# Second projection of a dense MLP as a Strassen block product over token, hidden and model halves

## Chip, cores and metric

The kernel runs on one core of one Trainium2 chip. The metric is the device time of one execution in microseconds (us), the median of several runs. TensorE (PE) multiplies, VectorE (DVE) and ScalarE (ACT) work elementwise, GpSimd (POOL) does small vector work and issues some transfers, SyncE (SP) issues most transfers.

## The reference, cut to what matters

Two blocks follow each other. The first has two layers, each with its mixers and then a dense MLP; the second has its own mixers and a mixture of experts. The change touches the MLP of the two layers of the first block, on 256 tokens, 1024 model columns and 4096 hidden columns (FF), all in fp32:

```python
def hybrid_layer(x, ...):            # twice
    ...
    x = x + mix @ w_out
    h2 = rms_norm(x, g_mlp_norm)
    x = x + jnp.square(jax.nn.relu(h2 @ w_up)) @ w_down   # w_up 1024x4096, w_down 4096x1024
    return x
```

The second block also needs, for each of its two layers, the product of a vector `c` with `ada_w` (1024x6144). It does not depend on x.

## The kernel before

**Tiles.** Tokens are two tiles t of 128. The MLP goes through eight units u of 512 hidden columns. For a unit, `mlp_up` (L815) fills PSUM banks 4 and 5 with the hidden values, transposed (hidden columns on partitions): 4 column groups of 128, 8 steps k each. ACT applies relu (L1558) and squares (L1560) into `uT`, a double buffer in `work`. `mlp_down` (L828) then adds this unit's share to the four PSUM banks 0 to 3, one for each token tile t and model half of 512 columns: 4 steps k for each bank, so 16 matmuls of 128x128 by 128x512. Each fp32 matmul stands in the trace as two instructions. The model rows are scaled by `rr` and added to `xres` only after all eight units.

**Order.** `MLP_ORDER` is up 0, up 1, down 0, up 2, down 1, ..., up 7, down 6, down 7; within an engine everything runs in the order it is written. Before down 7 PE does two small things: `ada_sum` (L838) and some transposes of parameter rows (L992, L993 in layer 1).

**Weights.** A unit of weights is 2 MB. Five slots of `ring` (0 to 4) hold them in turn; SP issues a load (L490) when the unit that used the slot five places earlier is done.

**What DVE does meanwhile.** In both layers DVE computes one half of the `ada_w` product during the MLP: 12 blocks c of 512 columns. A block is 1024x512 values, 2 MB, in two halves of 1 MB in slot 5 of the ring. POOL issues each half (L688) as soon as DVE is through with the one before in that place (semaphore `ada_acc`). For a block DVE does one TENSOR_SCALAR (L2223), seven SCALAR_TENSOR_TENSOR (L2225), a transpose (L2237, or L2235 for four blocks) and a reduction (L2239). At the end of the MLP it adds the product to `xres` (L2259 for tile 0, L2263 and L2265 for the halves of tile 1).

**After layer 1** the second block begins: DVE takes sums of squares (L1984), POOL makes the factor from them (L705, L707), ACT scales tile 0 (L1599) and DVE tile 1 (L1996), PE transposes both (L1020) and starts on the second block's first projection (L1042). POOL writes some constants for the second block (L695 to L697) once the semaphore `x_done` is at 5, which it is before the MLP of layer 1 begins.

Of the kernel before, what the change touches and what calls it, by code (L numbers as in the profile page):

```python
# [9 lines left out]
ALU = mybir.AluOpType  # L10
# [19 lines left out]
RING1, UNIT = 5, 4096  # L30
ROWS_BANK = (3, 7)
U_QK, U_R0, U_R1, U_R2, U_V, U_LORA, U_O, U_OUT, U_MLP = 0, 1, 2, 3, 4, 5, 6, 7, 9
UNITS1 = 25
MLP_ORDER = [("up", 0)] + [x for u in range(1, 8) for x in (("up", u), ("down", u - 1))] + [("down", 7)]
# [86 lines left out]
def first_and_second_block(nc, a, out, stop=None, dbg=None):  # L121
# [8 lines left out]
    with ctx:  # L130
# [17 lines left out]
        trig = first_only(8 * TT * 24).rearrange("p (i t j) -> p i t j", i=8, t=TT)  # L148
        ada_bias = first_only(L2 * 48).rearrange("p (l n) -> p l n", l=L2)
# [26 lines left out]
        def take(n, place=None):  # L176
# [32 lines left out]
        uT = work[:, 0:2048].rearrange("p (b c s) -> p b c s", b=2, c=4)  # L209
        ru = work[:, 2048:3072].rearrange("p (b n) -> p b n", b=2)  # L210
        ada_w = [ring[:, 5, 0:2048].rearrange("p (k n) -> p k n", k=4), ring[:, 5, 2048:4096].rearrange("p (k n) -> p k n", k=4)]
        ada_acc = work[:, 3072:4096].rearrange("p (b n) -> p b n", b=2)
        rr = sb("rr", [P, TT])[:, :]
        ada_t = work[:, 4096:4608]
        ada_red = work[:, 4608:4608 + 192].rearrange("p (c b) -> p c b", c=12)
# [5 lines left out]
            "consts", "pool_own", "params_p", "params_first", "cols_ps", "cols_sb", "x_in", "x_half", "xT_filled", "xT_act", "xT_dve", "diag_r", "rbc_filled", "out_half", "down_half", "tokens_pos", "trig_dve", "trig_act", "cond_act",  # L221
# [5 lines left out]
            "up_filled", "up_square", "down_done", "ada_acc", "ada_red", "ada_filled",  # L227
            "dve_own", "act_own", "passed", "stored")}
        ada_in = [sem("ada_in0"), sem("ada_in1")]
# [14 lines left out]
        def slot(j):  # L244
            return ring[:, j % RING1, :]

        def wide(j, n, k=DT):
            return slot(j)[:, 0:k * n].rearrange("p (k n) -> p k n", k=k)

        uq = slot(U_LORA)[:, 0:3 * 384].rearrange("p (k n) -> p k n", k=3)  # L250
        ukv = slot(U_LORA)[:, 1152:1152 + 1024].rearrange("p (k n) -> p k n", k=2)


# [18 lines left out]
        def unit_done(l, p):  # L272


            first, p = (0, p + UNITS1) if p < 0 else (1, p)
            if p < U_OUT:
                return "job_filled", NJ * l + JOB[{U_QK: "qk1", U_R0: "r01", U_R1: "r11", U_R2: "r21", U_V: "v1", U_LORA: "lkv1", U_O: "o1"}[p]] + 1
            if p < U_MLP:
                return ("out_filled", l + 1) if p == U_OUT else ("out_half", 4 * l + 4)
            kind, u = MLP_ORDER[p - U_MLP]  # L280
# [31 lines left out]
        rowsA = region(0, 128)  # L312
        rowsB = region(128, 128)
# [55 lines left out]
        landed2 = landed + [sem("landed5")]  # L369
        base2 = [16 * L1 * (UNITS1 // RING1 + (1 if r == U_LORA % RING1 else 0)) for r in range(RING1)] + [0]  # L370
# [52 lines left out]
        def _(sp):  # L423
# [43 lines left out]
            for l in range(L1):  # L467

                loads = [(wide(U_QK, 512), w_in[l, :, :, 0:512])]
# [4 lines left out]
                for i, (kind, u) in enumerate(MLP_ORDER):  # L474
                    loads.append((wide(U_MLP + i, 512), w_up[l, :, :, 512 * u:512 * u + 512]) if kind == "up" else
                                 (wide(U_MLP + i, 1024, 4), w_down[l, u]))
# [240 lines left out]
        def _(pe):  # L717
# [88 lines left out]
            def mlp_up(l, i, u):  # L806
                unit(l, U_MLP + i)
                w = wide(U_MLP + i, 512)
                for b in range(2):
# [7 lines left out]
                    if b == 0:  # L817
                        last.then_inc(s["up_filled"], 1)
# [1884 lines left out]
```

## Time and profile before

| | us |
|---|---|
| median of 3 runs | 2043.9 (2043.49 to 2044.44) |
| span of the profiled execution, first to last instruction | 2039.9 |
| PE busy in it | 1983.3 (97%) |
| DVE busy in it | 900.6 (44%) |
| ACT busy in it | 375.7 (18%) |
| POOL busy in it | 89.3 (4%) |

The profile gives the profiled execution's span; what lies around it (loading, the end) is the difference of some 4.0 us to the median. The chain of work that ended last runs over PE for 91% of the span: 11% on L815 (the first projection), 11% on L828 (the second). The idle time of an engine matters only where it stands on this chain. In the rows below, starts are us from the start of the span; "ns" stands where a duration is in ns.

### The profile page before, as it was taken

The numbers are of one execution on the slowest core, as the hardware profiler recorded it, in microseconds if no ns is written. First come the engines' busy times: TensorE is split into PE (matmuls) and PEld (weight loads), VectorE is DVE, ScalarE is ACT, GpSimd is POOL, SyncE is SP. The second block draws the span as 40 slices with busy tenths as digits, with TensorE's granted clock in tenths as the row PEclk, the third lists the DMA queues.
The fourth block names the chain that finished last, engine by engine and source line by source line (L and its number), as shares of the span: only waits on it lengthen the run. The fifth ranks groups of instructions, "written<-read, shape, count | busy, mean of one in ns | idle before, by whom it ended". The sixth has DMA issues, their size and how long they took to land.

```text
span 2039.9 us, 21592 instructions
## 1 busy us (share of the span) xinstructions
PE 1983.3 (97%) x8174; PEld 1097.2 (54%) x8174; DVE 900.6 (44%) x1828; ACT 375.7 (18%) x783; POOL 89.3 (4%) x167
## 2 busy tenths in 40 slices
PE   8999999999999999899999999989998999999997
PEld 5556666545666658654444344447765443444442
DVE  3354561245354419866777665661525110011102
ACT  2321000033100001122111111112342211111111
POOL 1121110001111000000000000000000000000000
PEclk9999999999999999989999999999999999999999
DMA  7327885333488733549999999993244999999995
GB/s 269 143 98 268 312 319 203 137 124 124 162 316 321 283 133 115 198 166 409 428 428 428 428 427 429 426 370 122 99 165 165 408 409 427 428 426 427 426 427 237
DMA packets 111572, 593.12 MB, mean 291 GB/s; under 512 B 16887, under 2 KB 21494, under 8 KB 85110
## 3 DMA queue, kind: packets, MB, share of 16 engines
q1 hardware_dynamic: 98422, 541.48, 66.1%
q0 software_dynamic: 13056, 50.33, 6.5%
q8 instruction: 66, 1.08, 0.2%
q14 instruction: 28, 0.23, 0.0%
HBM read 590.74 MB, written 1.05 MB: 290 GB/s over the span
## 4 chain that ended last, share of the span: by engine, by line
PE 91%; DMA 3%; DVE 3%; POOL 1%; issue 1%; ACT 1%; SPq 0%; POOLq 0%; DVEq 0%; ACTq 0%
PE bank L1169 31%; PE bank L815 11%; PE bank L828 11%; PE bank L1042 7%; PE bank L751 6%; PE bank L1160 5%; PE bank L1144 5%; DMA ring<-in_moe_w_up 3%; PE bank L954 3%; PE bank L1062 2%; PE bank L863 1%; PE bank L1312 1%; PE bank L1152 1%; POOL rstd L678 1%; PE bank L1330 1%
## 5 line engine op out<-in xcount | busy, mean ns | idle before, releaser
L1169 PE MATMUL bank<-ring,work 128*64 128x512 f32 x2336 | 634.8, 595 | 6.0 <-DMA ring<-in_moe_w_up 5.9
L1169 PEld LDWEIGHTS bank<-ring,work 128*64 128x64 f32 x2336 | 204.4, 137 | 329.8 <-issue 329.6
L2507 DVE SCALAR_TENSOR_TENSOR work<-work 128x512 f32<-128x512 f32 x384 | 258.6, 745 | 5.1 <-DVE work L2504 5.0
L815 PE MATMUL bank<-hT,ring 128*128 128x256 f32 x1024 | 223.4, 379 | 0.7 <-ACT hT L1470 0.7
L828 PE MATMUL bank<-ring,work 128*128 128x512 f32 x512 | 222.4, 592 | 0.0
L815 PEld LDWEIGHTS bank<-hT,ring 128*128 128x128 f32 x1024 | 194.4, 190 | 32.6 <-issue 6.9
L2511 DVE SCALAR_TENSOR_TENSOR work<-work,bank 128x512 f32<-128x512 f32 x32 | 21.9, 685 | 375.2 <-ACT work L1674 375.2
L1169 PE MATMUL bank<-seventh,work 128*64 128x512 f32 x400 | 176.1, 593 | 0.0
L2225 DVE SCALAR_TENSOR_TENSOR work<-ring,seventh,work 128x512 f32<-128x512 f32 x168 | 126.3, 752 | 109.5 <-DMA ring<-in_ada_w 104.3
L828 PEld LDWEIGHTS bank<-ring,work 128*128 128x128 f32 x512 | 97.2, 190 | 115.6 <-issue 114.8
L1042 PE MATMUL bank<-hT,ring 128*128 128x256 f32 x608 | 137.8, 388 | 0.3 <-ACT hT L1584 0.3
L751 PE MATMUL bank<-ring,hT 128*128 128x512 f32 (+1 forms) x320 | 135.0, 579 | 0.0
L1042 PEld LDWEIGHTS bank<-hT,ring 128*128 128x128 f32 x608 | 117.7, 195 | 19.5 <-issue 3.1
L1160 PE MATMUL bank<-work 128*128 128x512 f32 x256 | 123.4, 606 | 0.0
L1169 PE MATMUL bank<-work 128*64 128x512 f32 x256 | 114.7, 594 | 0.0
L1144 PE MATMUL bank<-work,xn 128*128 128x256 f32 x448 | 99.0, 379 | 0.0
L751 PEld LDWEIGHTS bank<-ring,hT 128*128 128x128 f32 x320 | 59.8, 190 | 68.7 <-issue 68.5
L1144 PEld LDWEIGHTS bank<-work,xn 128*128 128x128 f32 x448 | 84.0, 190 | 10.8
L1169 PEld LDWEIGHTS bank<-seventh,work 128*64 128x64 f32 x400 | 54.1, 137 | 57.8 <-issue 57.6
L1558 ACT ACTIVATE work<-bank 128x512 f32<-128x512 f32 x32 | 19.1, 597 | 347.4 <-PE bank L815 347.4
L1160 PEld LDWEIGHTS bank<-work 128*128 128x128 f32 x256 | 44.0, 191 | 57.5 <-issue 56.6
L2517 DVE SCALAR_TENSOR_TENSOR work<-work,bank 128x512 f32<-128x512 f32 x32 | 22.0, 688 | 114.1 <-PE bank L1169 114.1
(391 smaller groups left out, 1743.3 us busy)
## 6 DMA issues: line engine op xcount, KB each, us to landing
ring<-in_moe_w_gate SPq DMA_DIRECT2D x54, 2048.0 KB, 17.1
ring<-in_moe_w_up SPq DMA_DIRECT2D x45, 2048.0 KB, 19.4
ring<-in_moe_w_down SPq DMA_DIRECT2D x45, 2048.0 KB, 19.0
ring<-in_ada_w POOLq DMA_DIRECT2D x48, 1024.0 KB, 9.1
ring<-in_w_up SPq DMA_DIRECT2D x16, 2048.0 KB, 12.7
ring<-in_w_down SPq DMA_DIRECT2D x16, 2048.0 KB, 9.7
ring<-in_w_in SPq DMA_DIRECT2D x10, 2048.0 KB, 7.9
seventh<-in_moe_w_gate SPq DMA_DIRECT2D x10, 2048.0 KB, 19.7
```

The costliest lines, as they stand in the source:

```text
L751: last = pe.matmul(b[:, 0:n], (hT if x is None else x)[:, k, t * P:t * P + P], w[:, k, 0:n], start=(k == kk - 1), stop=(k == 0))
L815: last = pe.matmul(B(4 + b)[:, (c % 2) * S:(c % 2) * S + S], w[:, k, c * P:c * P + P], hT[:, k, :], start=(k == 0), stop=(k == DT - 1))
L828: last = pe.matmul(B(2 * t + hf), uT[:, u % 2, k, t * P:t * P + P], w[:, k, 512 * hf:512 * hf + 512], start=(u == 0 and k == 0), stop=(u = ...
L954: last = pe.matmul(B(2 * t + hf), mT[:, 4 * u + k, t * P:t * P + P], w[:, k, 512 * hf:512 * hf + 512], start=(u == 0 and k == 0), stop=(u ...
L1042: last = pe.matmul(b[:, (c % 2) * S:(c % 2) * S + S], w[:, k, c * P:c * P + P], hT[:, k, :], start=(k == 0), stop=(k == DT - 1))
L1062: last = pe.matmul(B(2 * t + hf), x[:, 4 * u + k, t * P:t * P + P], w[:, k, 512 * hf:512 * hf + 512], start=(u == 0 and k == 0), stop=(u = ...
L1144: last = pe.matmul(b[:, (d % 2) * S:(d % 2) * S + S], xn[:, t, d * P:d * P + P], pick[:, t, :], start=(t == 0), stop=(t == TT - 1))
L1160: last = pe.matmul(B(2 * t + hf), pgT[:, t * P:t * P + P], ye[:, 512 * hf:512 * hf + 512], start=False, stop=True, skip_group_check=True)
L1169: last = pe.matmul(b[h, :], x[:, k, h], rows_of(i, j + e, k)[:, c0:c0 + 512], start=(k == 0), stop=(k == kk - 1))
L2225: ins = dve.scalar_tensor_tensor(ada_acc[:, c % 2, :], ada_w[hf][:, k, :], cond[:, kk:kk + 1], ada_acc[:, c % 2, :], ALU.mult, ALU.add)
L2507: mo.do(dve.scalar_tensor_tensor(fl(bias[:, h]), mask_b, rbt[:, bass.ds(12 * bk + h, 1)], fl(bias[:, h]), ALU.mult, ALU.add))
L2517: dve.scalar_tensor_tensor(aa, zz, 0.5, U, ALU.mult, ALU.mult).then_inc(m["a_ready"], 1)
```

## The change

The second projection is written as a Strassen (Winograd form) product of 2x2 blocks, over the halves of the tokens (the tiles t), of the hidden columns (units u and u + 4) and of the model columns. For a pair pr = 0 to 3 of units pr and pr + 4, seven products n = 1 to 7 of 4 matmuls each take the place of eight. Product n adds up over the four pairs in a PSUM bank of its own, so seven banks are taken and the eighth (bank 7) takes the hidden values.

- DVE makes the factors. For each pair, four operations on weights of 128x2048 (`weights`, the 1st reads both second-projection units, the 2nd writes in place into the ring) and four on hidden values of 128x512 (`tokens`).
- PE's order (`MLP_STEPS`): four fills (half a first-projection unit each, 16 matmuls) for pair 0; then for each next pair its four fills, between them the seven products of the pair before in the order 6, 7, 4, 5, 3, 1, 2; last the seven products of pair 3 in the order 6, 1, 5, 7, 2, 3, 4. `ada_sum` stands ahead of these last seven.
- At the end DVE puts the seven sums together and adds them to `xres`.
- The ring's six slots all hold weights, with a slot for each unit by name (`UNITS1`): first-projection units 0 to 3 all use slot 0, units 4 to 7 slot 1.
- The `ada_w` blocks come in quarters of 512 KB into four places (two in `xn`, two in `work`) instead of halves of 1 MB into two. DVE's factor operations stand among its twelve blocks: the weights of pair 0, blocks 0 and 1, tokens of pair 0, blocks 2 and 3 (3 with the weights of pair 1 after its quarters), 4 and 5, tokens of pair 1, and so on.
- POOL writes the constant columns of `qkpad` and `vext` again after layer 0. Its constants for the second block now wait for `x_done` at 6, the last addition of layer 1.

```diff
-RING1, UNIT = 5, 4096
+RING1, UNIT = 6, 4096
-MLP_ORDER = [("up", 0)] + [x for u in range(1, 8) for x in (("up", u), ("down", u - 1))] + [("down", 7)]
+UNITS1 = [("qk", 0, 1), ("r0", 1, 1), ("r1", 2, 1), ("r2", 3, 1), ("v", 4, 1), ("lora", 0, 2), ("o", 1, 1), ("out0", 2, 1), ("out1", 3, 1),
+          ("down1", 4, 1), ("up0", 0, 1), ("down5", 5, 1), ("up4", 1, 1), ("down0", 2, 1), ("down4", 3, 1),
+          ("up1", 0, 1), ("up5", 1, 1), ("up2", 0, 1), ("up6", 1, 1), ("down2", 2, 1), ("down6", 3, 1),
+          ("up3", 0, 1), ("up7", 1, 1), ("down3", 4, 1), ("down7", 5, 1)]
+FILL_BANKS = (4, 5, 6, 7, 4)
+SUM_BANK = {1: 4, 2: 0, 3: 1, 4: 2, 5: 6, 6: 5, 7: 3}
+BETWEEN = ((6, 7), (4,), (5,), (3,), (1, 2))
...
-        ada_w = [ring[:, 5, 0:2048].rearrange("p (k n) -> p k n", k=4), ring[:, 5, 2048:4096].rearrange("p (k n) -> p k n", k=4)]
+        ada_w = [xn[:, q, :].rearrange("p (k n) -> p k n", k=2) for q in range(2)]
+        ada_w += [work[:, 4096 + 1024 * q:5120 + 1024 * q].rearrange("p (k n) -> p k n", k=2) for q in range(2)]
...
+        def factors(pr, n):
+            return {1: (hidden_of(pr, 0, 0), quarter(pr, 0, 0)),
+                    2: (hidden_of(pr, 0, 1), quarter(pr, 1, 0)),
+                    3: (usum[4], quarter(pr, 1, 1)),
+                    4: (hidden_of(pr, 1, 1), wdiff[4]),
+                    5: (usum[1], quarter(pr, 0, 1)),
+                    6: (usum[2], wdiff[2]),
+                    7: (hidden_of(pr, 1, 0), wdiff[3])}[n]
...
+            kind, u = name[:-1], int(name[-1])
             if kind == "up":
-                return "up_filled", 16 * (l + first) + 2 * u + 2
-            return ("down_half", 4 * (l + first)) if u == 7 else ("down_done", 7 * (l + first) + u + 1)
+                return "up_filled", 16 * l + 4 * (u % 4) - (2 if u < 4 else 0)
+            return "sums", sums_of(l, u % 4 - 2, 2)
...
                 for c in range(12):
-                    for hf in range(2):
-                        pool.wait_ge(s["ada_acc"], 24 * l + 2 * c + hf + 1)
-                        pool.dma_start(ada_w[hf], ada_src[l, :, 4 * hf:4 * hf + 4, 512 * c:512 * c + 512]).then_inc(ada_in[hf], 16)
+                    for q in range(4):
+                        pool.wait_ge(s["ada_acc"], 48 * l + 4 * c + q + 1)
+                        pool.dma_start(ada_w[q], ada_src[l, :, 2 * q:2 * q + 2, 512 * c:512 * c + 512]).then_inc(ada_in[q], 16)
...
-            pool.wait_ge(s["x_done"], 5)
+            pool.wait_ge(s["x_done"], 6)
...
+            def mlp_sum(l, pr, n):
+
+                if n in (3, 5, 6, 7):
+                    pe.wait_ge(s["factors_ready"], 32 * l + 8 * pr + {5: 5, 6: 6, 7: 7, 3: 8}[n])
+                if n == 4:
+                    pe.wait_ge(s["factors_ready"], 32 * l + 8 * pr + 4)
+                if n in (1, 2, 3):
+                    unit(l, "down%d" % (pr if n == 1 else pr + 4))
+                x, w = factors(pr, n)
+                for k in range(4):
+                    last = pe.matmul(B(SUM_BANK[n]), x[:, k, :], w[:, k, :], start=(pr == 0 and k == 0), stop=(pr == 3 and k == 3), skip_group_check=True)
+                last.then_inc(s["sums"], 1)
...
+                for n in (3, 1, 2, 4):
+                    weights(0, n)()
+                ada_block(0)
+                ada_block(1)
+                tokens(0)
+                for pr in range(1, 4):
+                    c = 4 * pr - 2
+                    ada_block(c)
+                    ada_block(c + 1, [weights(pr, n) for n in (3, 1, 2, 4)])
+                    if pr < 3:
+                        ada_block(c + 2)
+                        ada_block(c + 3)
+                    tokens(pr)
...
+                dve.wait_ge(s["sums"], sums_of(l, 3, 2))
+                do(added(0, low, bank_of(2)))
+                dve.wait_ge(s["sums"], sums_of(l, 3, 3))
+                ins = added(0, high, bank_of(3))
+                wait()
+                ins.then_inc(s["x_half"], 1)
+                dve.wait_ge(s["x_half"], 2 * l + 2)
+                if l == L1 - 1:
+                    r[0] = squared(0, xn[:, 0, :])
+                dve.wait_ge(s["sums"], sums_of(l, 3, 4))
+                added(1, low, bank_of(4)).then_inc(s["x_done"], 1)
```

PE, where the second projection begins in layer 0; before, L815 is the first projection and L828 the second:

```order
L815 MATMUL bank<-hT,ring 128x256 [waits up_square,landed0]
L815 MATMUL bank<-hT,ring 128x256 x15
L815 MATMUL bank<-hT,ring 128x256 [waits up_square]
L815 MATMUL bank<-hT,ring 128x256 x15
L828 MATMUL bank<-ring,work 128x512 [waits up_square,landed1]
L828 MATMUL bank<-ring,work 128x512 x15
L815 MATMUL bank<-hT,ring 128x256 [waits up_square,landed2]
L815 MATMUL bank<-hT,ring 128x256 x15
```

The same place in the changed kernel, where L880 is a fill and L893 a product:

```order
L880 MATMUL bank<-hT,ring 128x256 [waits up_square,landed0]
L880 MATMUL bank<-hT,ring 128x256 x15
L893 MATMUL bank<-work 128x512 [waits factors_ready]
L893 MATMUL bank<-work 128x512 x3
L893 MATMUL bank<-work 128x512 [waits factors_ready]
L893 MATMUL bank<-work 128x512 x3
L893 MATMUL bank<-work 128x512 [waits factors_ready]
L893 MATMUL bank<-work 128x512 x3
L880 MATMUL bank<-hT,ring 128x256 [waits up_square]
L880 MATMUL bank<-hT,ring 128x256 x15
L893 MATMUL bank<-ring,work 128x512 [waits factors_ready]
L893 MATMUL bank<-ring,work 128x512 x3
```

The runs of 16 of the second projection have become runs of 4 (products 6, 7, 4, then 5), of which each waits for DVE's `factors_ready`, where the 16 waited for ACT alone.

DVE, from the factor `rr` of layer 0's MLP to the end of the first `ada_w` block, before:

```order
L2214 TENSOR_TENSOR rr<-rstd 128x2 [waits rstd_ready,stat_ready]
L2223 TENSOR_SCALAR work<-ring,seventh 128x512 [waits ada_in0,dve_own]
L2225 SCALAR_TENSOR_TENSOR work<-ring,seventh,work 128x512 [waits dve_own] x3
L2225 SCALAR_TENSOR_TENSOR work<-ring,seventh,work 128x512 [waits ada_in1,ada_acc]
L2225 SCALAR_TENSOR_TENSOR work<-ring,seventh,work 128x512 [waits dve_own] x3
L2237 STREAM_TRANSPOSE work<-work 128x512 [waits ada_acc]
L2239 TENSOR_REDUCE work<-work 128x16 [waits dve_own]
```

And in the changed kernel, from the same `rr`; `landed2` and `landed3` are the units down0 and down4:

```order
L2281 TENSOR_TENSOR rr<-rstd 128x2 [waits rstd_ready,stat_ready]
L2333 TENSOR_TENSOR work<-ring 128x2048 [waits landed3,landed2,dve_own]
L2336 TENSOR_TENSOR ring<-ring 128x4x512 [waits factors_ready]
L2341 TENSOR_TENSOR work<-ring 128x2048 [waits factors_ready]
L2346 TENSOR_TENSOR work<-ring,work 128x2048 [waits factors_ready]
L2292 TENSOR_SCALAR work<-xn,seventh 128x512 [waits ada_in0,factors_ready]
L2294 SCALAR_TENSOR_TENSOR work<-xn,seventh,work 128x512 [waits dve_own]
L2294 SCALAR_TENSOR_TENSOR work<-xn,seventh,work 128x512 [waits ada_in1,ada_acc]
L2294 SCALAR_TENSOR_TENSOR work<-xn,seventh,work 128x512 [waits dve_own]
L2294 SCALAR_TENSOR_TENSOR work<-work,seventh 128x512 [waits ada_in2,ada_acc]
```

Four operations of 128x2048 now stand ahead of the first block, behind a wait for a weight unit, and the block waits for four transfers where it waited for two.

POOL, ahead of the second block's first factor, in the changed kernel (before, the IOTA row has no other wait than `x_done` either, at a lower value):

```order
L759 IOTA work 128x32 [waits x_done]
L760 MEMSET work 128x4x2
L761 MEMSET work 128x4x30
L769 TENSOR_SCALAR stat<-stat 128x1 [waits pool_own,stat_ready_2]
L771 TENSOR_TENSOR rstd<-stat,mhalf 128x1 [waits pool_own]
```

The order of these rows is unchanged; the value waited for is that of the end of layer 1's MLP, so the first factor (tile 0) stands behind it.

## Rows read from the trace of the kernel before

**Rows 1.** The page: the span, and the busy time of DVE.

```profile
span 2039.9 us, 21592 instructions
PE 1983.3 (97%) x8174; PEld 1097.2 (54%) x8174; DVE 900.6 (44%) x1828; ACT 375.7 (18%) x783; POOL 89.3 (4%) x167
```

**Rows 2.** The chain that ended last, in both MLPs: start, us, what.

```profile
165.75 27.87 PE bank L815 x128
193.62 13.73 PE bank L828 x32
207.35 13.81 PE bank L815 x64
...
748.31 13.75 PE bank L828 x32
```

**Rows 3.** Busy time by stretch; the last columns are granted clock, DMA share, GB/s.

```profile
193.50:221.00 27.50, 27.50 (x97) 18.20 (x96) 15.68 (x23) 2.45 (x4) 2.99 (x4) 1.00 0.94 347
```

**Rows 4.** Timeline of DVE in layer 0: start, us, line, operation, idle before it.

```profile
160.12 1.22 DVE L2202 TENSOR_TENSOR xres<-xres,bank 128x1024 f32<-128x1024 f32 x1 [8.90 <-PE bank L954]
...
163.55 0.69 DVE L2206 TENSOR_TENSOR xres<-xres,bank 128x512 f32<-128x512 f32 x1 [1.03 <-PE bank L954]
...
176.44 0.48 DVE L2223 TENSOR_SCALAR work<-ring,seventh 128x512 f32<-128x512 f32 x1 [5.96 <-DMA ring<-in_ada_w]
176.96 2.33 DVE L2225 SCALAR_TENSOR_TENSOR work<-ring,seventh,work 128x512 f32<-128x512 f32 x3
182.37 3.11 DVE L2225 SCALAR_TENSOR_TENSOR work<-ring,seventh,work 128x512 f32<-128x512 f32 x4 [3.09 <-DMA ring<-in_ada_w]
185.52 0.71 DVE L2237 STREAM_TRANSPOSE work<-work 128x512 f32<-128x512 f32 x1
186.26 0.69 DVE L2239 TENSOR_REDUCE work<-work 128x16 f32<-128x512 f32 x1
...
321.03 0.69 DVE L2239 TENSOR_REDUCE work<-work 128x16 f32<-128x512 f32 x1
372.99 0.17 DVE L2249 TENSOR_TENSOR modc<-bank,seventh 32x24 f32<-32x24 f32 x1 [51.28 <-PE bank L838]
```

**Rows 5.** Timeline of POOL in layer 0: the first two issues of `ada_w`.

```profile
170.16 1.74 POOL L688 DMA_DIRECT2D ring<-in_ada_w  x2
```

**Rows 6.** Line L688: the 48 issues of `ada_w` and their time to landing.

```profile
L688 POOL DMA_DIRECT2D ring<-in_ada_w x48: 748/748/954, 170.2 to 692.9; - x48
...
DMA to landing us min/median/max: 5.5/9.1/12.0
```

**Rows 7.** Loads of `w_down` issued from 100 to 165 us.

```profile
L490 SPq DMA_DIRECT2D ring<-in_w_down x1: 368/368/368, 122.8 to 122.8; - x1
...
DMA to landing us min/median/max: 7.7/7.7/7.7
```

**Rows 8.** All loads of `w_up`, and their time to landing.

```profile
L490 SPq DMA_DIRECT2D ring<-in_w_up x16: 368/368/368, 91.7 to 665.0; - x16
...
DMA to landing us min/median/max: 8.2/12.7/15.3
```

**Rows 9.** The page: ACT's relu, mean ns of one.

```profile
L1558 ACT ACTIVATE work<-bank 128x512 f32<-128x512 f32 x32 | 19.1, 597 | 347.4 <-PE bank L815 347.4
```

**Rows 10.** Timelines of POOL and of all engines, end of layer 1's MLP.

```profile
693.63 0.18 POOL L695 IOTA work<- 128x32 f32 x1
...
758.76 1.15 ACT L1599 ACTIVATE xn<-xres,rstd 128x1024 f32<-128x1024 f32 x1 [10.02 <-POOL rstd L707]
...
761.89 1.04 PE L1020 MATMUL bank<-ident,xn 128*128 128x128 f32 x8
...
762.09 0.75 DVE L2265 SCALAR_TENSOR_TENSOR xres<-bank,rr,xres 128x512 f32<-128x512 f32 x1 [2.60 <-PE bank L828]
...
764.57 0.56 POOL L707 TENSOR_TENSOR rstd<-stat,mhalf 128x1 f32<-128x1 f32 x1
...
766.04 1.37 PE L1020 MATMUL bank<-ident,xn 128*128 128x128 f32 x8 [3.12 <-DVE xn L1996]
```

More of the change, by code:

```diff
@@ L481, in _ @@
+                for u in range(8):
+                    loads["up%d" % u] = (512, DT, w_up[l, :, :, 512 * u:512 * u + 512])
+                    loads["down%d" % u] = (1024, 4, w_down[l, u])
+                for j, (name, z, _) in enumerate(UNITS1):
+                    if l > 0 or j >= 5:
+                        kind, value = slot_free(l, name)
                         sp.wait_ge(s[kind], value)
                         stand(sp, s["passed"])
-                    if j == U_OUT + 1 + RING1 and l + 1 < L1:
+                    if name == "lora":
+                        sp.dma_start(uq, w_uq[l]).then_inc(landed[z], 16)
+                        sp.dma_start(ukv, w_ukv[l]).then_inc(landed[z], 16)
+                    else:
+                        n, k, src = loads[name]
+                        sp.dma_start(wide(name, n, k), src).then_inc(landed[z], 16)
+                    if name == "down4" and l + 1 < L1:
@@ L728, in filled, with unit @@
                 ins.then_inc(s["job_filled"], 1)
-            def unit(l, j):
-                n = (2 if j == U_LORA else 1)
-                per = UNITS1 // RING1 + (1 if j % RING1 == U_LORA % RING1 else 0)
-                k = j // RING1 + (1 if j % RING1 == U_LORA % RING1 and j >= U_LORA else 0) + 1
-                pe.wait_ge(landed[j % RING1], 16 * per * l + 16 * k)
+            def unit(l, name):
+                z, value = landed1(l, name)
+                pe.wait_ge(landed[z], value)
             def transposes(l, names, src, dst_cols):
@@ new lines, in bank_of, with added @@
+                def bank_of(n):
+                    return B(SUM_BANK[n])
+                def added(t, c, src):
+                    return dve.scalar_tensor_tensor(xres[:, t, c], src, rr[:, t:t + 1], xres[:, t, c], ALU.mult, ALU.add)
+                r = [None, None]
+                dve.wait_ge(s["sums"], sums_of(l, 3, 1))
+                do(dve.tensor_copy(mlp_w[:, 0, :], bank_of(1)))
+                wait()
+                do(dve.tensor_tensor(mlp_w[:, 1, :], bank_of(6), mlp_w[:, 0, :], ALU.add))
@@ new lines, in _ @@
+                do(added(0, low, mlp_w[:, 0, :]))
+                wait()
+                dve.wait_ge(s["sums"], sums_of(l, 3, 5))
+                do(dve.tensor_tensor(mlp_w[:, 2, :], bank_of(5), mlp_w[:, 1, :], ALU.add))
+                wait()
+                do(added(0, high, mlp_w[:, 2, :]))
+                dve.wait_ge(s["sums"], sums_of(l, 3, 7))
+                do(dve.tensor_tensor(mlp_w[:, 3, :], bank_of(7), mlp_w[:, 1, :], ALU.add))
+                wait()
+                do(added(1, low, mlp_w[:, 3, :]))
@@ new lines, in _ @@
+                do(dve.tensor_tensor(mlp_w[:, 0, :], bank_of(5), mlp_w[:, 3, :], ALU.add))
+                wait()
+                do(added(1, high, mlp_w[:, 0, :]))
+                dve.wait_ge(s["sums"], sums_of(l, 3, 2))
+                do(added(0, low, bank_of(2)))
+                dve.wait_ge(s["sums"], sums_of(l, 3, 3))
+                ins = added(0, high, bank_of(3))
+                wait()
+                ins.then_inc(s["x_half"], 1)
+                dve.wait_ge(s["x_half"], 2 * l + 2)
```

347 lines of the change are left out of this document (199 added, 148 removed).

## Prediction

> **What bounds the kernel now.** I read the page first: DVE is busy for 44% of the span, PE for 97% [rows 1]. Then the chain of work that ended last: through both MLPs it is PE and nothing else, and the reader is to see that its pieces touch. The second projection starts at 193.62 and takes 13.73 us, and the next piece starts at 207.35, so a satisfied wait between two pieces costs nothing [rows 2]. Layer 0's MLP lasts from 165.75 to 387.1, 221.3 us. The table by stretch says what else is near a limit: in 193.5 to 221 the transfers move 347 GB/s at a share of 0.94, DVE is busy for 15.7 of 27.5 us, the clock is at 1.00 (2.4 GHz) [rows 3]. So PE decides, transfers are close behind, and DVE has room if its data come.
>
> **What is removed.** A unit of the second projection is 16 matmuls, 32 instructions, 13.73 us [rows 2]: 0.858 us a matmul. A product of the change is four, 3.43 us. A layer had 8 units, 128 matmuls; it gets 4 pairs x 7 products x 4 = 112. Sixteen fewer are 13.7 us a layer, 27.5 us for two. The fills are the 64 half-pieces of before in other banks: 13.81 us a unit [rows 2], no change. Operand shapes are the same, so I take the same price per matmul.
>
> **What is added, on DVE.** Per pair, four operations of 128x2048, all operands in SBUF. No row has one. TENSOR_TENSOR of 512 took 0.69, of 1024 1.22 [rows 4]: 0.53 per 512, so 2.29, and 2.33 with the step to the next. The other end is SCALAR_TENSOR_TENSOR, 0.78 per 512 [rows 4], or 3.1; I take 2.33, being the same operation as in the rows. Four are 9.3 us. The token operations are 0.73 each, 2.9 for four, of which the first two (1.5 us) release product 6. Per pair 12.2 us, per layer 49. DVE's `ada_w` work in a layer is 12 blocks. Without waits a block takes 0.52 + 2.37 + 3.15 + 0.74 + 0.6 = 7.4 us [rows 4], 7.8 in the four with the longer transpose; with its waits it took 12.1, since twelve ran from 176.44 to 321.7 [rows 4]. DVE then idled for 51.28 us [rows 4]. 12 x 7.5 + 49 = 139 us of DVE fit easily into 208. The sum doesn't decide, though. The order does: PE waits for factors that stand behind blocks, and blocks wait for transfers.
>
> **The timetable.** Count from the first matmul of the MLP (165.75 in layer 0; layer 1 is alike). PE without a stall: fills of pair 0 until 27.7, the first fill of pair 1 until 34.6, then product 6 of pair 0. From pair 1 on, a pair is four fills and seven products, 27.6 + 24.0 = 51.6 us. Product 6 of pair 1 is due at 79.3 (three products, a fill, one, a fill, one, a fill, two), that of pair 2 at 131, that of pair 3 at 182.5, and the end, with the small pieces ahead of the last products, at 207.6, 13.7 below 221.3.
> DVE: `rr` is done near 4.6. Unit down4 can be loaded once the output projection is done, near -2, and a load that met little traffic landed in 7.7 [rows 7], so the weights start at about 6 and are done at 15.5. Let b be the mean time of a block, waits for transfers in it. The first two token operations of pairs 0, 1, 2 are then done at
> - 17.0 + 2b, due at 34.6: stall from b = 8.8;
> - 29.2 + 6b, due at 79.3: stall from b = 8.4;
> - 41.4 + 10b, due at 131: stall from b = 9.0.
> Pair 3 has only two blocks ahead of it, 53.6 + 12b, and 182.5 to meet; it is safe up to b = 10.8. The squares are no limit: fill 4 of a pair ends two products, 6.9 us, ahead of product 6, against two passes of ACT of 0.6 each [rows 9] and 1.5 us of DVE.
>
> **What b will be.** Its floor is 7.5. Before, a half of 1 MB landed 9.1 us after its issue in the median, 5.5 at best [rows 6]; the place was refilled only after DVE's 3.1 us, and 9.1 + 3.1 is the 12.1 seen. So b was the refill cycle of one place. With quarters, a place is free for refill after 1.6 us, all four are requested while the block is used up, and the first block is issued from 170.2 [rows 5] and landed long before the weights of pair 0 are done. While DVE makes factors, the four places fill. If quarters still took 9.1 us, a free-running cycle would be 9.1 + 1.6 = 10.7; half the bytes behind the same number of bytes in flight should take less, nearer the 5.5. Bandwidth allows that: 347 GB/s at a share of 0.94 is 369 at full share [rows 3]. Up to 74 DVE needs six blocks, 12.6 MB, and PE has asked for three first-projection units, 6.3 MB: 51 us of transfers, 70 at hand. Up to 126 it is ten blocks and seven units, 35.7 MB: 97 us of 121. In the stretch after pair 0's products end (79.3), units down2 and down6 are asked for only then and pair 2's weights wait for them, at up to 12 us for two [rows 7, 8] some 5 to 9 us of DVE, but that place has 10 us of room, and the next block's quarters fill meanwhile. I take b = 7.9 to 8.3: no stall, with little to spare at pair 1.
>
> Unit up1 takes slot 0 from up0 at 13.8 and is due at 27.7: 13.9 us. Loads of `w_up` took 8.2 to 15.3 [rows 8], so 0 to 1.4 us a layer; the `w_down` load that ran beside the slowest is no longer there, so I take 0. Product 4 of pair 3 ends the MLP with one addition of 0.75 behind it, as before [rows 10]; the others are done under the products ahead. Writing `qkpad` and `vext` again is two small POOL operations, hidden behind the next layer's start.
>
> **The end of layer 1.** POOL's constants (0.18 for the first, some 0.4 in all) now come after the last addition, 0.95 us after PE's end at 761.9, and tile 0's factor stands behind them. Factor (about 0.85, with 0.56 for its last step), ACT 1.15 and PE 1.04 for eight transposes [rows 10] put tile 0's transposes at 3.6 to 4.65 after PE's end, where they were done at once. Tile 1's began 4.15 after it [rows 10]. So 0.5 us is lost.
>
> **Sum.** -27.5 + 0.5 = -27.0 against the span of 2039.9: 2012.9. The median is 4.0 above the span, so 2016.9. For the hand-overs from DVE to PE, which no row prices, I add 0.5 a layer: 2018.
>
> **A rule against it.** Two halves in flight landed in 9.1, and 1 MB never faster than 5.5 [rows 6]. The Trainium skill (DMA: Bandwidth & Descriptors, on the two cost components) gives a transfer from GpSimd's queue about 2.0 us fixed plus bytes over 436 GB/s. By it 1 MB takes 4.4 us and 512 KB 3.2, an estimate; four of them not overlapped make a block of 12.8 us, and b would stay above 12, the slower rival below. The trace has transfers overlapping at 347 GB/s, so I don't follow it. A second one bears on the same queue. POOL's 48 issues took 748 ns, at most 954, while DVE ran operations with two SBUF inputs beside them [rows 6]. The Trainium skill (SBUF — State Buffer, two separate sides) has an exclusive port pair for which such operations and GpSimd can block each other; longer operations of 2.3 us would delay each issue by up to that, and the row shows no such delay.
>
> **Rivals.**
> - *Transfers of quarters stay slow, PE waits a little.* If a quarter lands in 9 us, b is 9 to 10 with the cover that the factors give. At b = 9.5 the stalls by the three lines are 1.4, 6.9 and 5.4; the largest counts, since each delay moves the later dues. 6.9 a layer gives 2018 + 14 = 2032. For it: DVE waited for `ada_w` at nearly each block before. Against it: the cover, and the bandwidth left. This starts at b = 8.4.
> - *DVE's chain becomes the bound, slower than before.* b stays at 12.1, set by the queue, and factors come on top. The third line gives 41.4 + 121 = 162.4, a stall of 31.4 a layer against 13.7 saved: +17.7 a layer, 2018 + 63 = 2081. The place is product 6 of pair 2; it is slower than before from 10b + 41.4 = 144.7, b = 10.3.
> - *The products cost more than a quarter unit.* A wait for DVE at each product, or another bank every four matmuls. Before, the bank changed every four matmuls too and the pieces touched [rows 2]. At 0.1 us for each of 56 products: 2024.
>
> **How the numbers follow.** Forecast (PE with under 2 us of stall a layer, 2016.5 to 2021): 0.6. Waits of 2 to 10 us a layer, or dearer products, 2021 to 2038: 0.27. Near no change: 0.05. Slower, 2048 to 2085: 0.08. The low end is the sum without the extra, 2016; the high end reaches into the first rival until 2 in 10 are left out: 2031. About 0.2% (4 us) is what a measurement of this kernel can tell from no change: faster by more 0.87, within 0.05, slower 0.08.
>
> **What would show it.** In the changed kernel's chain, products in pieces of 3.43 and fills of 6.9 that touch, and an MLP of 207 to 209 us. Idle time of the product line put down to DVE would show the first rival; its sum is the stall. DVE's 128x2048 rows should be near 2.29. The landing of the 96 quarters should have a median below 7. The prediction is wrong if DVE still waits for `ada_w` when the last fill of pair 1 ends, and if up1 isn't there at 27.7.

## The result, and the profile after

| | before | after |
|---|---|---|
| median of 6 runs, us | 2044.17 (2043.49 to 2046.16) | 2038.03 (2037.31 to 2041.21) |
| span of the profiled execution | 2039.9 | 2036.3 |
| PE busy in it | 1983.3 | 1962.3 |
| DVE busy in it | 900.6 | 1007.6 |

The ratio after to before, estimated from the single runs, is 0.9964, with a 95% interval from 0.9955 to 0.9974 (the quotient of the two medians is 0.9970). The change saves some 6 to 7 us where 26 were forecast: the sign was right, the size wrong by a factor of about four, and 2038.03 lies above the range's 2031.

The page of the kernel after, the span and the busy times, against [rows 1]:

```profile
span 2036.3 us, 21726 instructions
PE 1962.3 (96%) x8110; PEld 1087.0 (53%) x8110; DVE 1007.6 (49%) x1910; ACT 376.0 (18%) x783; POOL 123.6 (6%) x217
```

PE is busy for 21 us less, DVE for 107 more. So PE's work is gone, but most of its time was not saved: it turned into waiting. The chain that ended last shows where, in layer 0 (start, us, what; L880 is a fill, L893 a product), against [rows 2]:

```profile
201.38 10.30 PE bank L893 x24
...
239.27 6.88 PE bank L893 x16
246.75 23.41 DMA ring<-in_w_down
270.35 2.30 DVE work L2333
...
292.62 8.75 DMA work<-in_ada_w
306.23 9.41 PE bank L893 x16
...
361.14 24.05 PE bank L893 x56
```

Products and fills touch until 246.15, the end of pair 0's products, as forecast. (PE itself works on without a gap until 297.80; the chain follows only what ended last.) Then the chain leaves PE: over the transfer of a second-projection unit, DVE's first weight operation of pair 2, a quarter of `ada_w`, and back to PE at 306.23. That is product 6 of pair 2. PE's and DVE's timelines give the two waits (in brackets, idle time ahead and what ended it), first PE's two, then DVE's two, in layers 0 and 1:

```profile
306.23 9.41 PE L893 MATMUL bank<-work 128*128 128x512 f32 x16 [8.43 <-DVE work L2359]
675.96 8.86 PE L893 MATMUL bank<-work 128*128 128x512 f32 x16 [5.91 <-DVE work L2359]
```

```profile
270.35 2.29 DVE L2333 TENSOR_TENSOR work<-ring 128x2048 f32<-128x2048 f32 x1 [13.81 <-DMA ring<-in_w_down]
641.12 2.29 DVE L2333 TENSOR_TENSOR work<-ring 128x2048 f32<-128x2048 f32 x1 [14.88 <-DMA ring<-in_w_down]
```

DVE stood 13.8 and 14.9 us in front of units down2 and down6; everything queued behind on DVE moved, PE waited 8.4 and 5.9 us, and the 16 instructions behind each wait took 9.4 and 8.9 us where 16 others took 6.9.

**The books.** By the chains of the two profiles, the MLP of layer 0 took 218.6 us (166.61 to 385.19) against 221.3, that of layer 1 215.6 (538.87 to 754.45) against 221.4. That is 8.5 off where 27.5 were to go. The missing 19.0 us are, to 0.2 us, the two waits (14.3) and the slow instructions behind them (2.5 + 2.0).

Behind layer 1 the gap from PE's last product to the second block's first projection grew from 5.7 to 7.7 us. The stretch ahead of the first MLP is 0.9 longer, the one between the two MLPs 0.1, the rest of the second block 2.0, 1274.1 against 1272.2. The change puts no work into these three. The 0.9 is no property of it: in the trace of e1_late below the first MLP begins at 165.78, as before (165.75). The 2.0 is within what single executions differ by: in the traces of the kernels below the same rest takes 1272.7 to 1276.3 us. The sum, -8.5 + 2.0 + 0.9 + 0.1 + 2.0, is with rounding the -3.6 between the two spans. The medians are 6.1 apart. In a later set an execution of the kernel before took 2045.6 with a span of 2043.5, so what lies around the span is 2.1, and not 4.0 as I had taken; by that the span of 2039.9 belongs to an execution shorter than any of the six in the table, but its own time is not on record.

### The profile page after: what moved, and what is told of

It reads as the page before. It is cut to its first block, busy times and chain, and to the rows that moved or that the text cites. A ratio compares the mean times of both kernels' runs of the same rounds, so it can differ in the third digit from the quotient of the medians.

```text
span 2036.3 us, 21726 instructions
## 1 busy us (share of the span) xinstructions
PE 1962.3 (96%) x8110; PEld 1087.0 (53%) x8110; DVE 1007.6 (49%) x1910; ACT 376.0 (18%) x783; POOL 123.6 (6%) x217
## 4 chain that ended last, share of the span: by engine, by line
PE 84%; DMA 7%; DVE 6%; POOL 1%; issue 1%; ACT 1%; SPq 0%; DVEq 0%; POOLq 0%; ACTq 0%
PE bank L1234 30%; PE bank L880 8%; PE bank L893 7%; PE bank L1107 7%; PE bank L812 6%; PE bank L1209 5%; PE bank L1225 5%; DMA ring<-in_moe_w_up 3%; PE bank L1017 3%; PE bank L1127 3%; DMA ring<-in_w_down 2%; PE bank L926 1%; PE bank L1377 1%; DVE work L2294 1%; DMA seventh<-in_moe_w_up 1%
## 5 line engine op out<-in xcount | busy, mean ns | idle before, releaser
L880 PE MATMUL bank<-hT,ring 128*128 128x256 f32 x1024 | 225.1, 379 | 0.7 <-ACT hT L1534 0.7
L880 PEld LDWEIGHTS bank<-hT,ring 128*128 128x128 f32 x1024 | 194.4, 190 | 36.9 <-issue 11.7
L1225 PE MATMUL bank<-work 128*128 128x512 f32 x256 | 123.4, 606 | 0.0
L893 PE MATMUL bank<-ring,work 128*128 128x512 f32 x256 | 113.9, 592 | 0.0
L893 PE MATMUL bank<-work 128*128 128x512 f32 x192 | 89.2, 616 | 14.3 <-DVE work L2359 14.3
L769 POOL TENSOR_SCALAR stat<-stat 128x1 f32<-128x1 f32 (+1 forms) x12 | 4.2, 347 | 1263.2 <-ACT work L1779 951.2
L2294 DVE SCALAR_TENSOR_TENSOR work<-work,seventh 128x512 f32<-128x512 f32 x96 | 72.2, 752 | 10.5 <-DMA work<-in_ada_w 7.4
```

Source lines behind the costliest of these rows:

```text
L880: last = pe.matmul(b[:, (c % 2) * S:(c % 2) * S + S], w[:, k, c * P:c * P + P], hT[:, k, :], start=(k == 0), stop=(k == DT - 1))
L893: last = pe.matmul(B(SUM_BANK[n]), x[:, k, :], w[:, k, :], start=(pr == 0 and k == 0), stop=(pr == 3 and k == 3), skip_group_check=True)
L1225: last = pe.matmul(B(2 * t + hf), pgT[:, t * P:t * P + P], ye[:, 512 * hf:512 * hf + 512], start=False, stop=True, skip_group_check=True)
L2294: ins = dve.scalar_tensor_tensor(ada_acc, ada_w[q][:, k, :], cond[:, kk:kk + 1], ada_acc, ALU.mult, ALU.add)
```

## The experiments

Two theories for the missing 14 to 19 us. **W**: one in-order wait on DVE for two units asked for late. **B**: DVE's work and the `ada_w` stream together are too much, wherever the wait stands. And **C**, for the part behind the waits: PE's clock falls when PE idles. All ratios are to the kernel before in the same set. The later sets' medians of before were 2045.6 (e1 to e4), 2045.9 (e5 to e8) and 2046.2 (e9, e10), so kernels of different sets are compared by ratio.

| kernel | edit to the changed kernel | median, us | ratio (95%) |
|---|---|---|---|
| after | none | 2038.03 | 0.9964 (0.9955 to 0.9974) |
| e1_late | pair 2's weights in block 9 | 2019.33 | 0.9864 (0.9848 to 0.9881) |
| e2_down_first | down2, down6 asked for ahead of up6 | 2023.93 | 0.9896 (0.9879 to 0.9912) |
| e4_filler | PE kept busy in the wait | 2035.05 | 0.9946 (0.9926 to 0.9966) |
| e3_half_ada | half the bytes of `ada_w`, so half its product is left out | 2022.93 | 0.9886 (0.9865 to 0.9907) |
| e8_block8 | pair 2's weights in block 8 | 2022.08 | 0.9873 (0.9850 to 0.9896) |
| e7_halves | e1_late with 1 MB halves | 2043.67 | 0.9985 (0.9974 to 0.9996) |
| e5_pool | POOL's constants later | 2032.65 | 0.9926 (0.9900 to 0.9952) |
| e6_late_pool | e1_late and e5_pool | 2018.51 | 0.9865 (0.9846 to 0.9885) |
| e10_late_pool_again | the same again | 2017.19 | 0.9860 (0.9843 to 0.9876) |
| e9_busy_gap | the same, PE kept busy after layer 1 | 2017.98 | 0.9862 (0.9845 to 0.9878) |

### The place of the wait: e1_late, e8_block8

```diff
-                    ada_block(c + 1, [weights(pr, n) for n in (3, 1, 2, 4)])
+                    own_weights = [weights(pr, n) for n in (3, 1, 2, 4)]
+                    ada_block(c + 1, () if pr == 2 else own_weights)
                     if pr < 3:
                         ada_block(c + 2)
-                        ada_block(c + 3)
+                        ada_block(c + 3, own_weights if pr == 2 else ())
```

> One edit to the changed kernel: the four weight operations of pair 2 stand in block 9 instead of block 7, so that the wait for units down2 and down6 comes some 20 us later; nothing else moves. Theory W (the stall of 8.4 and 6.0 us at product 6 of pair 2 comes from DVE standing 13.8 us in front of two units that are asked for late): idle time of PE before that product under 1 us a layer, the slow matmuls behind it gone too (some 2.5 and 2 us), so about 19 us off: near 2019. Theory B (VectorE's work and the ada_w stream together are too much for the first 140 us of the MLP, wherever the wait stands): the blocks wait for ada_w instead, 4 us or more of stall a layer stay, 2028 to 2038.

Measured: 2019.33. In the chain of e1_late, the last two products of pair 1 and the first two of pair 2 touch again around 297 (13.73 us, 32 instructions in one piece), and the last seven products of layer 0 start at 349.34 and take the 24.05 us of the sum:

```profile
290.10 13.73 PE bank L893 x32
303.83 6.91 PE bank L880 x32
...
349.34 24.05 PE bank L893 x56
```

Layer 0's MLP takes 207.6 us (165.78 to 373.39), the figure of the timetable, and layer 1's 207.7. W holds. What B had right shows in DVE's waits from 170 to 309 us (total, times, longest), first of the kernel after, then of e1_late:

```profile
DVE work L2333 <- DMA ring<-in_w_down: 16.7, 2, 13.8
DVE work L2294 <- DMA work<-in_ada_w: 5.3, 6, 2.1
DVE work L2294 <- DMA xn<-in_ada_w: 1.3, 2, 0.9
```

```profile
DVE work L2294 <- DMA work<-in_ada_w: 5.0, 6, 1.2
DVE work L2294 <- DMA xn<-in_ada_w: 4.0, 3, 1.8
DVE work L2292 <- DMA xn<-in_ada_w: 3.5, 2, 2.1
DVE work L2333 <- DMA ring<-in_w_down: 2.9, 1, 2.9
```

With the 13.8 gone, waits for `ada_w` rose from 6.9 (with 0.3 at L2292) to 12.5: some of the long wait had been prefetching for the blocks behind it. So moving it won 8.2 us of DVE time, not 13.8, and that was just enough: product 6's factor came 129 us after the MLP's start, due at 131. DVE still waits 10.1 and 12.0 us for the units of pair 3 (8.5 and 8.6 in the kernel after), and that costs PE nothing: what decides is when the result is due, not how long DVE waits.

The same edit with block 8 in place of 9 gives the dose:

> The changed kernel with the weight operations of pair 2 in block 8, between the place they have (7) and that of the version that lost the stall (9). Theory W: DVE comes to the wait 8 us later, so it waits about 6 instead of 13.8 us, and the factor of product 6 comes at 131 to 133 us after the MLP's start against 139.6 (due at 131): stall 0 to 2 us a layer, time 2019 to 2024. Theory B: at most half of the stall goes, 2028 or more.

Measured: 2022.08; DVE waited 6.0 at that place, PE 2.04 and 1.60 us. These are the numbers of W, the first of PE's waits at the edge. The four times lie from 2018.7 to 2025.8, too far apart to tell this kernel from e1_late (the two intervals overlap), so the dose is shown by the waits: 13.8, 6.0 and none for DVE, 8.4, 2.0 and none for PE.

### What stands ahead of the two units: e2_down_first, e3_half_ada

```diff
-          ("up1", 0, 1), ("up5", 1, 1), ("up2", 0, 1), ("up6", 1, 1), ("down2", 2, 1), ("down6", 3, 1),
+          ("up1", 0, 1), ("up5", 1, 1), ("up2", 0, 1), ("down2", 2, 1), ("down6", 3, 1), ("up6", 1, 1),
```

> One edit to the changed kernel: SyncE asks for down2 and down6 ahead of up6, which was asked for 7 us before them and landed after 16 us. Theory W with the transfers limited by bandwidth (about 370 GB/s): 2 MB less ahead of the two, some 5.7 us, so DVE waits about 8 instead of 13.8 us, the stall falls to 2 to 3 and 0 to 1 us, time near 2024. Rival: the 23 us from issue to landing are set by something else than what is queued ahead (the ada_w queue, HBM): the wait stays at 12 or more, time 2034 to 2040.

In the kernel after, SP asked for up6 at 239.38 and for the pair at 246.26:

```profile
239.38 0.37 SPq L545 DMA_DIRECT2D ring<-in_w_up  x1
246.26 1.04 SPq L545 DMA_DIRECT2D ring<-in_w_down  x2
```

From 239.4 to the second unit's landing at 270.2 three units of 2.1 MB and eight quarters of `ada_w` (4.2 MB, the first of them asked for 0.6 us earlier) were asked for: 10.5 MB in 30.8 us, 341 GB/s. The trace has 354 GB/s moved in this stretch, at a share of 0.94. e2_down_first came out at 2023.93 as W had it, with 18.90 us from issue to the landing of the second unit instead of 23.41, and PE waits of 1.63 and 2.17 (forecast 0 to 1 for the second). One part missed: DVE's wait fell only to 12.01 in layer 0 and 14.00 in layer 1, not to 8, which is where the rival had it. In layer 0 DVE reached the place 2.8 us sooner (253.7 against 256.5), since the quarters of block 6 came faster as well, so part of the gain stands in other rows than the wait. The landing, PE's waits and the time speak for W.

```diff
-                        pool.dma_start(ada_w[q], ada_src[l, :, 2 * q:2 * q + 2, 512 * c:512 * c + 512]).then_inc(ada_in[q], 16)
+                        pool.dma_start(ada_w[q][:, 0:1, :], ada_src[l, :, 2 * q:2 * q + 1, 512 * c:512 * c + 512]).then_inc(ada_in[q], 16)
```

> The changed kernel with half of the ada_w data: each quarter loads only its first row group, 256 KB, and DVE reads this one twice; as many transfers and operations as before, half the bytes, so part of the ada_w product is left out. Theory W, bandwidth: down2 and down6 land in about 17 us after their issue instead of 21 to 23, DVE waits about 8 instead of 13.8, the stall is 0 to 3 us a layer, time near 2022. Rival (the weight units' own queue is the limit): landing over 20 us, time 2034 or more.

Measured: 2022.93 (two runs), the landing 17.94 us, DVE's wait 12.21 again because DVE came sooner, PE's wait 0.24 in layer 0 and none in layer 1. This run also takes away nearly all of DVE's waits for `ada_w` (0.9 us are left of 6.9), so its time alone doesn't tell the two streams apart; the landing does. Less of either stream brings the units sooner and cures most of the stall, so the 23 us are what two streams make of shared bandwidth. By landing and time the rivals of both runs fall.

### The clock behind the wait: e4_filler

```diff
+                    if (pr, i) == (2, 6):
+                        pe.wait_ge(s["up_square"], 16 * l + 12)
+                        for _ in range(6):
+                            pe.matmul(B(7), hT[:, 0, 0:P], hT[:, 0:2, :].rearrange("p k s -> p (k s)"), start=True, stop=True)
                     mlp_sum(l, pr, i)
```

> The changed kernel with six matmuls of 128x512 into the free bank 7 (result unused) ahead of product 6 of pair 2, in the time in which PE stood idle. Theory C (after an idle stretch PE runs at a lower granted clock for some us, which costs 2.5 us in layer 0 and about 2 in layer 1 on top of the wait): the 16 instructions behind the wait take 6.9 instead of 9.4 us, the wait itself shrinks by what the six take (5.1 us), time 3 to 5 us lower, near 2034. Rival (the slow records come from something that begins when the products begin, such as DVE working beside them): they stay at 9.4, and the time stays at 2038.

Table by stretch of the kernel after: PE's wait and what follows (the last three columns are granted clock, DMA share, GB/s). Behind it the same of e4_filler:

```profile
290.00:297.80 7.80, 7.80 (x21) 3.52 (x19) 6.78 (x9) 1.23 (x2) 2.66 (x5) 1.00 0.89 305
297.80:306.20 8.40, 0.00 (x0) 0.00 (x0) 6.10 (x9) 0.00 (x0) 1.88 (x3) 0.67 1.03 391
306.20:312.00 5.80, 5.77 (x8) 2.52 (x9) 5.52 (x9) 0.00 (x0) 1.45 (x2) 0.60 1.03 401
```

```profile
297.00:303.50 6.50, 5.38 (x13) 2.09 (x11) 4.59 (x7) 0.00 (x0) 1.45 (x2) 1.00 1.02 382
303.50:310.00 6.50, 6.45 (x15) 2.96 (x16) 6.22 (x9) 0.00 (x0) 1.86 (x3) 1.00 1.03 400
```

After 8.4 us without work the granted clock averages 0.60 over the next 5.8 us, a mix of 1.2 and 2.4 GHz; with six matmuls in the wait it stays at 1.00, and the 16 instructions take 7.13 us instead of 9.41. DVE and the transfers are as busy in both, so the rival falls for layer 0. In layer 1 the six ended too soon: PE still idled for 3.97 us and the 16 took 8.83. The time, 2035.05 and a ratio of 0.9946 against 0.9964, moved by 3.7 us, the forecast's size, but the two intervals overlap; what is shown is the clock, not the time. e2_down_first bears it out, with 7.13 us and a clock of 1.00 behind waits of 1.63 and 2.17; in e8_block8 a wait of 2.04 was followed by 8.83 us, at a clock of 0.66 in the first 5 us, so about 2 us of idle time can go either way.

### Whether the quarters matter: e7_halves

```diff
-                    for q in range(4):
-                        pool.wait_ge(s["ada_acc"], 48 * l + 4 * c + q + 1)
-                        pool.dma_start(ada_w[q], ada_src[l, :, 2 * q:2 * q + 2, 512 * c:512 * c + 512]).then_inc(ada_in[q], 16)
+                    for h in range(2):
+                        pool.wait_ge(s["ada_acc"], 48 * l + 4 * c + 2 * h + 2)
+                        pool.dma_start(ada_half[h], ada_src[l, :, 4 * h:4 * h + 4, 512 * c:512 * c + 512]).then_inc(ada_in[2 * h], 16)
```

> The version with pair 2's weights in block 9, but ada_w again in halves of 1 MB, two places, each asked for when both its quarters are used, as before the change. Theory (the block time b was the refill cycle of a place): b rises from 8.4 towards 10 to 12 us, DVE's factors of pair 1 come 5 to 15 us late, and the time is 2030 to 2060. Rival (b is set by the bandwidth, not by the number of places): waits for ada_w grow by less than 3 us a layer, time 2019 to 2024.

Measured: 2043.67, a ratio of 0.9985, 24 us over e1_late: nearly the whole gain is gone. DVE waited 23.0 us for `ada_w` from 170 to 309 against 12.5, and PE now waits at all three dues of the timetable:

```profile
201.21 10.57 PE L894 MATMUL bank<-work 128*128 128x512 f32 x24 [0.42 <-DVE work L2361]
248.52 8.83 PE L894 MATMUL bank<-work 128*128 128x512 f32 x16 [2.28 <-DVE work L2361]
305.78 8.83 PE L894 MATMUL bank<-work 128*128 128x512 f32 x16 [3.63 <-DVE work L2361]
```

6.3 us of waits in layer 0 cost another 4.2 in slow instructions (10.57 against 10.30, twice 8.83 against 6.86), and layer 1 is much the same (waits of 0.40, 2.27 and 3.92). These two layers explain some 21 us. The profiled execution took 2038.03, the shortest of ten, 18 us over that of e1_late; of what the others took beyond it there is no trace. The time and the longer waits are those of the theory, and the rival of this run, bandwidth alone, falls. Two sizes missed: b, worked out from product 6's factor, was 8.9 at pair 1 and 9.8 at pair 2, not 10 to 12, and pair 1's factors came some 3 us after their due of 79.3, not 5 to 15. Since the edit makes the transfers larger and the places fewer at once, the run does not tell these two apart.

### The end of layer 1: e5_pool, e6_late_pool, e9_busy_gap, e10_late_pool_again

```diff
-            pool.wait_ge(s["x_done"], 6)
-            own.do(pool.iota(bno, ...))
...
             for n, (cols, width) in enumerate(STATS2):
                 power2(n, cols, width)
+                if n == 1:
+                    pool.wait_ge(s["x_done"], 6)
+                    own.do(pool.iota(bno, ...))
...
```

> The changed kernel with only the POOL edit: the second block's first two factors ahead of the constants. Theory: 1.5 to 2 us off, near 2036, the gap from the last product of layer 1 to the first projection of the second block 5.7 instead of 7.7 us. Rival: no change in the gap.

> The version with the weight operations of pair 2 in block 9, and in addition POOL makes the second block's first two factors before it writes its constants. In the changed kernel the second block's first projection begins 7.7 us after PE's last product of layer 1, before the change 5.7; POOL's constants and a first factor of 0.69 + 0.58 us stood in front of tile 0. Theory: without them tile 0 is ready before PE ends, and the 2.0 us come back: near 2017.5, 1.5 to 2 us under the version without this edit. Rival: the wait is for tile 1 anyway, as before the change: under 0.5 us.

The gap did what was expected: in e5_pool the last product ends at 754.78 and the second block's first projection begins at 760.42, 5.6 us; in e6_late_pool it is 5.65, against 7.7 and, in e1_late, 7.1. The time did not follow: 1.5 to 2 us under e1_late were expected, and e6_late_pool has the ratio of e1_late. In its trace that projection's 320 instructions took 72.28 us instead of 69.83, with a granted clock of 0.50 in the first 4 us, so here the gap's gain came back as a lower clock. e5_pool's ratio, 0.9926, is 7.8 us under that of the kernel after, much more than the gap; its four runs lie at 2029 and 2036 in pairs. Its trace is of 2035.91 and has the stall of the kernel after, with slower instructions behind shorter waits:

```profile
306.14 10.13 PE L894 MATMUL bank<-work 128*128 128x512 f32 x16 [7.54 <-DVE work L2360]
675.26 9.89 PE L894 MATMUL bank<-work 128*128 128x512 f32 x16 [4.56 <-DVE work L2360]
```

What the runs at 2029 did otherwise, no trace shows; that part stays open.

```diff
+                    if nth == 0 and t == 0:
+                        for _ in range(3):
+                            pe.matmul(B(0), hT[:, 0, 0:P], hT[:, 0:2, :].rearrange("p k s -> p (k s)"), start=True, stop=True)
```

> The version with pair 2's weights in block 9 and POOL's constants later, and in addition three matmuls of 128x512 (result unused, bank 0) between the transposes of tile 0 and tile 1 at the start of the second block, where PE waited some 3 us for tile 1. In the version without them the gap shrank from 7.1 to 5.65 us, but the 320 instructions of the first projection behind it took 72.3 instead of 69.8 us, with a granted clock of 0.50 in their first 4 us. Theory C (the clock falls after an idle stretch and costs what the gap had given): with PE busy the first projection takes 69 to 70 us, the clock there 1.00, and the time falls by 2 to 3 us, near 2015.5. Rival (the low clock there has another cause): no change, 2018 to 2019.

> The version with pair 2's weights in block 9 and POOL's constants later, without the three matmuls, again, to stand on the same chip as the one with them: 2018.5.

Tables by stretch, the first 4.5 us of that projection, of e9_busy_gap and of e10_late_pool_again:

```profile
740.00:744.50 4.50, 3.89 (x19) 3.33 (x18) 4.36 (x12) 1.55 (x4) 0.00 (x0) 1.00 1.03 403
```

```profile
740.00:744.50 4.50, 3.89 (x12) 3.05 (x11) 4.36 (x12) 1.51 (x4) 0.00 (x0) 0.62 1.06 406
```

The clock is at 1.00 with PE kept busy, against 0.62, and the projection takes 69.31 us against 70.99. The times, 2017.98 and 2017.19, don't differ, which is what the rival had: 1.7 us is less than these runs can tell. Theory C holds for the clock, and its price in the time isn't measured.

Counted from PE's last product of layer 1 to the end of that projection, the traces have 76.2 us before, 77.0 in the kernel after, 76.9 in e1_late, 77.9 and 76.6 in the two traces of the kernel with POOL's edit (e6, e10), and 75.4 in e9_busy_gap. So the 2.0 us of the gap cost 0.9 to the end of the projection: in the kernel after the low clock falls on the 16 transposes (0.57 from 758.5 to 761.9) and the projection behind them starts at 1.00, while before it falls on the projection (0.50 in its first 2 us).

## Why the prediction was wrong, point by point

- **What is removed**: right. The last seven products, 56 instructions, take 24.05 us in both layers, 3.44 a product, and with the stall removed a layer's MLP is 207.6 us.
- **DVE's operations**: right. The 128x2048 operation took 2.29 us, the value worked out from the two shorter ones; the four token operations 2.7.
- **The quarters**: right. Their landing had a median of 6.8 us, below the 7 that was named.
- **The timetable**: right in form. DVE's own work puts product 6's factor of pair 2 at 139.6 - 23.6 of waits = 116.0 us. In the term 41.4 + 10b, b was 8.44 without the weight wait (forecast 7.9 to 8.3) and 9.8 with it. Put into the line, 9.8 gives the stall that came, 8.4. The first rival forecast nearly this time, 2032, by this line at b = 9.5, but from another cause, quarters that land in 9 us.
- **The step that failed** is the sentence on pair 2's weights: "at up to 12 us for two [rows 7, 8] some 5 to 9 us of DVE, but that place has 10 us of room". Three sizes in it were wrong. The pair landed 23.4 us after its issue, since rows 7 and 8 are landings of single units and here up6 was still on its way and eight quarters came beside; at the 369 GB/s that I had myself, 10.5 MB are some 28 us. DVE waited 13.8. And the room, 131 - 41.4 - 10b, was about 10 only for b = 8.0; at 8.44 it is 5.2. 13.8 - 5.2 = 8.6 is, to 0.2 us, what PE waited. (Even 5.2 flatters it, for quarters landed during the long wait: in e1_late, with no wait at that place, the room left was 2 us.) I had reckoned bandwidth up to due times, where it fits, and not from the moment at which the slots become free. The overlap of that wait with PE's work is the step that failed; the rest of the path held.
- **The two signs of being wrong** that the prediction named did not come: DVE waits for no `ada_w` when the last fill of pair 1 ends (239.3 in layer 0; between 208.1 and 248.6 it waits for nothing), and up1 was there in time. They watched pair 1 and the quarters; the stall came at pair 2 and from the units.
- **A term that was missing**: the clock behind a stall, 2.5 and 2.0 us. Without a stall it is nothing, so the forecast's case didn't need it, but the rivals' prices and the range's upper end did.
- **The end of layer 1**: 0.5 forecast, 2.0 measured for the gap and 0.9 to the end of the projection behind it. The pieces of that forecast add up to 3.35 us for the start of tile 0's transposes (0.95 + 0.4 + 0.85 + 1.15), where it wrote 3.6; they began 4.05 us after PE's end, with POOL's first step at 0.69 us, not 0.19. And they ran at a lower clock: 16 took 3.36 us, where before they took 1.04 and 1.37 [rows 10].
- **The rivals**: "slower than before" did not come, but with halves (e7_halves) the change gives next to nothing. "The products cost more" fell: without a stall the pieces touch and cost 3.43 to 3.44 us a product.
- **up1**: PE waits for no landing in either MLP. That was right.
- **The offset of 4.0** between span and median came from comparing one execution's span with the median of others; where one execution has both, it is 2.1 us for the kernel before and 1.7 to 1.8 for the kernel after.

With pair 2's weight operations moved by two blocks (e1_late) the kernel takes 2019.3, in ratio 0.9864, which is 2016.4 on the first set's 2044.2. The prediction's sum was 2016.9, without its allowance for hand-overs. In differences: 27.0 us were to go, 27.8 went by the ratio and 26.3 by the medians of its set. That version, with or without POOL's edit, beats both kernels.

## What to carry to other kernels

When work is moved from a full engine to a half-idle one, ask not whether its share has room, but when each result is due and what stands ahead of it in that engine's order; here one in-order wait for a late transfer, placed one block after its issue instead of three, ate some 70% of the gain. Price such a wait from the moment of issue, with every byte then under way on all queues over the bandwidth that the trace shows, not with the landing time of a single transfer. And price a stall of PE above its length: the instructions behind it ran at a lower clock.

## What the runs showed of the hardware

- **The clock after idle time.** 16 product instructions took 6.86 us in the chain without a wait (the timeline, which lets neighbours overlap, has 7.03). They took 7.13 behind waits of 0.24 to 2.17 us, with the clock still at 1.00; 8.83 behind waits of 2.04 to 3.97, with 0.66 in the first 5 us of the shortest; 8.86 behind 5.91 and 9.41 behind 8.43; and, in e5_pool, 9.89 behind 4.56 and 10.13 behind 7.54, with 0.50 in the first 6 us. So a longer wait does not always cost more.
- **A POOL operation stretched beside a DVE operation.** The timeline of POOL in the kernel after, ahead of the second block:

```profile
755.92 0.69 POOL L769 TENSOR_SCALAR stat<-stat 128x1 f32<-128x1 f32 x1 [0.20 <-POOL work L761]
...
757.35 0.19 POOL L769 TENSOR_SCALAR stat<-stat 128x1 f32<-128x1 f32 x1
```

  The second one, with no DVE operation beside it, takes 0.19 us; the first ended at 756.61, just behind DVE's squares of 128x1024 (755.33 to 756.56). POOL's issues of `ada_w`, though, kept a median of 0.72 us beside DVE's operations of 2.29. The Trainium skill (SBUF — State Buffer, two separate sides) lets a DVE operation with two SBUF inputs block a POOL operation that reads SBUF, a condition that the prediction left out. The squares read `xres` for both inputs, and POOL's operation reads `stat`, so the 0.69 us agree with the page, in one place; the issues hardly changed, and no run shows whether they read SBUF at all.
- **Landing times under two streams.** A 2 MB unit landed in 7.7 us when little else moved [rows 7] and in up to 27.7 in the kernel after; 512 KB quarters in 4.2 to 12.1, with a median of 6.8. Before, halves of 1 MB took 5.5 to 12.0 [rows 6]: half the size, but not half the time.
